# A hybrid encoder layer on one core: attention-branch products and gates moved into the scan, elimination steps respread, and the last pair's sum made in PSUM

## The reference, cut to what matters

```python
h = rmsnorm(x, norm1_g) * (1.0 + sc1) + sh1
q, k, v, feat, gl = split(h @ w_in)
att = windowed_attention(q, k, v, attn_sink) @ w_br_attn
rw = rwkv7_bidir(feat, ...) @ w_br_rwkv          # forward scan + backward scan, group norm, bonus, * g
g_att, g_rw = split(sigmoid(gl))
x = x + gt1 * ((g_att * att + g_rw * rw) @ w_out)
h = rmsnorm(x, norm2_g) * (1.0 + sc2) + sh2
moe = expert_choice_moe(h, ...)                  # 16 experts, each takes its 64 best tokens
x = x + gt2 * moe
return rmsnorm(x, final_g)
```

## Time and profile before

| | us |
|---|---|
| three runs | 1594.44, 1598.31, 1598.44 (median 1598.31) |
| profiled execution | 1594.55, span 1592.7 |
| mean granted TensorE clock | 0.962 of 2.4 GHz |
| PE / DVE / ACT / POOL busy | 1402.1 / 467.1 / 205.3 / 39.1 |
| moved by DMA | 485.52 MB |

### The profile page before, as it was taken

How to read it: one execution, slowest core, us unless ns; L and a number is a source line. 1 busy time by engine, 2 the same in 40 slices (tenths; PEclk the granted TensorE clock), 3 DMA queues, 4 the chain that set the end, 5 groups by cost and what they waited for, 6 DMA issues and landing times.

```text
span 1592.7 us, 21565 instructions
## 1 busy us (share of the span) xinstructions
PE 1402.1 (88%) x9239; PEld 663.4 (42%) x9239; DVE 467.1 (29%) x807; ACT 205.3 (13%) x401; POOL 39.1 (2%) x45
## 2 busy tenths in 40 slices
PE   5988999899778998799979889989889989889886
PEld 1433544445676444434334343344343343343332
DVE  3799643762237323310200200200200200201103
ACT  2024001122223002101001001001010010010002
POOL 2003030000000000000000000000000000000000
PEclk9998999999899999799999999999999999999998
DMA  9951242144402173799999999999999999999995
GB/s 346 374 174 58 80 106 63 56 135 118 174 5 112 76 279 127 279 428 429 427 428 429 428 428 429 428 428 428 428 430 428 429 429 428 428 429 428 428 428 209
DMA packets 91267, 485.52 MB, mean 305 GB/s; under 512 B 36075, under 2 KB 53565, under 8 KB 62405
## 3 DMA queue, kind: packets, MB, share of 16 engines
q1 hardware_dynamic: 91149, 484.59, 74.8%
q10 hardware_dynamic: 56, 0.01, 0.0%
HBM read 470.93 MB, written 10.50 MB: 302 GB/s over the span
## 4 chain that ended last, share of the span: by engine, by line
PE 57%; DMA 29%; DVE 8%; issue 3%; POOL 1%; ACT 1%; SPq 1%; DVEq 0%; PEldq 0%; POOLq 0%
PE psum L1111 16%; DMA arena<-in_exp_w_up_dram 14%; DMA arena<-in_exp_w_gate_dram 12%; PE psum L1126 8%; PE psum L694 6%; PE psum L581 5%; PE psum L1092 4%; DMA arena<-in_ada_w_dram 4%; PE psum L997 3%; PE psum L1027 3%; PE psum L1200 2%; DVE arena L1611 1%; PE psum L709 1%; DVE arena L1479 1%; DVE inv_tmp L1609 1%
## 5 line engine op out<-in xcount | busy, mean ns | idle before, releaser
L1111 PE MATMUL psum<-arena 128*64 128x512 f32 x2048 | 474.2, 620 | 81.2 <-DMA arena<-in_exp_w_up_dram 62.3
L1111 PEld LDWEIGHTS psum<-arena 128*64 128x64 f32 x2048 | 165.8, 142 | 382.7 <-issue 382.4
L1126 PE MATMUL psum<-arena 128*64 128x512 f32 x992 | 217.5, 596 | 11.2 <-issue 9.4
L581 PE MATMUL psum<-arena 128*128 128x512 f32 x336 | 149.1, 605 | 1.4 <-DVE arena L1505 1.4
L1126 PEld LDWEIGHTS psum<-arena 128*64 128x64 f32 x992 | 83.5, 138 | 139.5 <-issue 139.3
L694 PE MATMUL psum<-arena 128*128 128x512 f32 x256 | 124.5, 610 | 0.0
L581 PEld LDWEIGHTS psum<-arena 128*128 128x128 f32 x336 | 64.5, 194 | 84.2 <-issue 80.6
L1881 DVE TENSOR_TENSOR arena<-arena,psum 128x512 f32<-128x512 f32 x32 | 19.8, 681 | 268.5 <-PE psum L1111 268.5
L1896 DVE TENSOR_TENSOR arena<-psum,arena 128x1024 f32<-128x1024 f32 x7 | 8.6, 1225 | 251.3 <-PE psum L1126 251.3
L1873 DVE TENSOR_TENSOR arena<-arena,psum 128x512 f32<-128x512 f32 x32 | 19.8, 681 | 169.3 <-ACT arena L1422 169.3
L1413 ACT ACTIVATE arena<-psum,arena 128x128 f32<-128x128 f32 x64 | 24.3, 457 | 328.6 <-PE psum L1092 328.6
(11 more groups left out here) (269 smaller groups left out, 1067.7 us busy)
## 6 DMA issues: line engine op xcount, KB each, us to landing
arena<-in_exp_w_gate_dram SPq DMA_DIRECT2D x64, 2048.0 KB, 24.5
arena<-in_exp_w_up_dram SPq DMA_DIRECT2D x64, 2048.0 KB, 26.7
arena<-in_exp_w_down_dram SPq DMA_DIRECT2D x62, 2048.0 KB, 26.9
arena<-in_ada_w_dram SPq DMA_DIRECT2D x24, 1024.0 KB, 9.9
arena<-in_w_in_dram SPq DMA_DIRECT2D x16, 1024.0 KB, 5.8
arena<-in_x_dram SPq DMA_DIRECT2D x2, 2048.0 KB, 8.5
gate_pre<-arena SPq DMA_DIRECT2D x16, 256.0 KB, 6.1
arena<-in_w_out_dram SPq DMA_DIRECT2D x1, 4096.0 KB, 20.9
```

The source lines that it names most:

```text
L581: ins = mm(bank(b % 4), by(w_ring[g % 2], KC)[:, k, j * P:(j + 1) * P], by(hT, KC)[:, k, :], start=(k == 0), stop=(k == KC - 1))
L1111: ins = mm(bank(4 * kind + n)[e * 64:(e + 1) * 64, :], by(xeT, KC)[:, k, e * 64:(e + 1) * 64], by(ring[(j + e) % RING], 2)[:, r, n * 512:( ...
L1126: ins = mm(bank(4 + n)[e * 64:(e + 1) * 64, :], by(hidT, FBLK)[:, 4 * kk + b, e * 64:(e + 1) * 64], by(ring[(j + e) % RING], 4)[:, b, n * ...
```

## The change

Seven things move.

1. Projection block 9 stands ahead of the sums of `kk` squares instead of behind them.
2. The triangle products of both directions are made together, two banks for each pair of chunks, and two gate products follow each of the four groups. Each query block then has 24 gate products; the heads of block q are turned inside block q+1, after its second pair of scores.
3. The elimination steps are spread over 24 places: four in the logits and eight in the heads of blocks 1 and 2.
4. In the scan both directions turn their keys through bank 6, so bank 7 is free. `att_branch` makes one attention-branch product at four places in each of steps 1 to 7, and four behind the scan. VectorE multiplies each block by its gate in place (`att_gated`), and ScalarE takes the sigmoids of the attention gates in steps 1 and 2.
5. `w_br_rwkv` goes to another place in SBUF and is loaded once the last `C` products (step 6 of the scan) are made, ahead of the second gate half; `g_spill` is loaded ahead of both.
6. Behind the scan the rwkv branch is made for the middle chunks first ("inner"), then for the outer ones; the mix has two operations a block instead of three.
7. In the last pair, tiles 0 to 2 of `x2` are put into PSUM by products with the identity; the put products add to them, and norm and final product read PSUM. Tile 3 is first and is summed by VectorE as before.

The diff, cut:

```diff
-        wba, wbr = at(136, 16 * KB), at(64, 16 * KB)
+        wba, wbr = at(136, 16 * KB), at(32, 16 * KB)
         wo = at(0, 32 * KB)
-        mix_tmp = [at(40, T), at(42, T)]
+        mix_tmp = at(64, T)
...
+            load(GG, g_spill, "g_moved")
+            sp.wait_ge(sem("C_mm"), 2 * STEPS)
+            sp.wait_ge(sem("N_mm"), 2 * STEPS - 2)
+            load(by(wbr, 4), w_br_rwkv[0].rearrange("(k p) n -> p k n", p=P), "wbr_in")
             load(by(gate_half[1], KC)[:, 0:4, :], gate_rows[:, KC:KC + 4, :], "gates_in")
-            load(GG, g_spill, "g_moved")
             sp.wait_ge(sem("Y_mm"), STEPS)
             load(by(gate_half[1], KC)[:, 4:KC, :], gate_rows[:, KC + 4:GATEB, :], "gates_in")
-            load(by(wbr, 4), w_br_rwkv[0].rearrange("(k p) n -> p k n", p=P), "wbr_in")
...
-            for b in range(7, 9):
+            for b in range(7, 10):
                 project(b)
             pe.wait_ge(sem("lora_out"), 19)
             pe.wait_ge(sem("kk_sq"), 1)
             for m in range(PAIRS):
                 ins = mm(bank(6)[m * 32:(m + 1) * 32, :], half_wide, by(kk_sq, PAIRS)[:, m, :], start=True, stop=True)
             ins.then_inc(sem("kk_sum"), 1)
-            for b in range(9, 12):
+            for b in range(10, 12):
...
+            def a_product(d, n, c, m, h):
+                left, right = ((al_, be_), (be_, al_))[d]
+                p = 1 - h if d == 0 else h
+                o = (c % 2 * PAIRS + m) * CHUNK
+                return mm(bank(4 + (2 * n + d) % 4)[head(p), o:o + CHUNK], left[head(h), d, m, token(c)],
+                          right[head(h), d, m, token(c)], start=True, stop=True)
+            pe.wait_ge(sem("v_nat_out"), 5)
+            for n in range(4):
+                if n >= 2:
+                    pe.wait_ge(sem("A_made"), 2 * n - 2)
+                for c in (2 * n, 2 * n + 1):
+                    for m in range(PAIRS):
+                        for h in range(2):
+                            a0 = a_product(0, n, c, m, h)
+                            a1 = a_product(1, n, c, m, h)
+                a0.then_inc(sem("A_mm"), 1)
+                a1.then_inc(sem("A_mm"), 1)
+                if n == 0:
+                    pe.wait_ge(sem("shift_done"), 13)
+                gate_products(2 * n, 2 * n + 2)
...
-                g0 = 26 * q
+                g0 = 8 + 24 * q
+                ahead, doubled = ((6, 2), (6, 2), (6, 2), (4, 0))[q]
-                gate_products(g0 + 8, g0 + 14)
+                    if q and j == 1:
+                        heads_turned(q - 1)
+                gate_products(g0 + 8, g0 + 8 + ahead)
+                g0 += 8 + ahead
...
-                    gate_products(g0 + 14 + h, g0 + 15 + h)
+                    more = 2 if h < doubled else 1
+                    gate_products(g0, g0 + more)
+                    g0 += more
-                gate_products(g0 + 22, g0 + 26)
-                pe.wait_ge(sem("o_ready"), q + 1)
-                if q:
-                    pe.wait_ge(sem("attT_ready"), q)
-                for m in range(4):
-                    ins = nc.tensor.transpose(bank(7)[:, m * P:(m + 1) * P], o_nat[:, m * P:(m + 1) * P], ident)
-                ins.then_inc(sem("attT_mm"), 1)
+            gate_products(100, 104)
+            heads_turned(TT - 1)
...
-                return mm(cell(6 + d, slot(h, d), m, 256 * n), (be_, ka_)[n][head(h), d, m, token(chunk(i, d))],
+                return mm(cell(6, slot(h, d), m, 256 * n), (be_, ka_)[n][head(h), d, m, token(chunk(i, d))],
...
+            def att_branch(b, m, k):
+                if k == 0 and b == 7 and m:
+                    pe.wait_ge(sem("mixT_ready"), m)
+                ins = mm(bank(b), by(wba, 4)[:, k, m * P:(m + 1) * P], by(attT, 4)[:, k, :], start=(k == 0), stop=(k == 3))
+                if k == 3:
+                    ins.then_inc(sem("mix_mm"), 1)
             Bq(0)
+            transposed(0, 0)
             for i in range(STEPS):
                 last = i == STEPS - 1
                 if i:
                     W_with_C(i, last)
                 else:
                     C(1, 0)
+                    transposed(0, 1)
                 if not last:
                     Bq(i + 1)
+                if i == 1:
+                    pe.wait_ge(sem("wba_in"), 16)
+                if i:
+                    att_branch(7, i - 1, 0)
                 U(i, 1)
                 U(i, 0)
                 if not last:
                     C_with_turns(i + 1)
                 if i > 5:
                     gn_transposed(i - 2)
+                if i:
+                    att_branch(7, i - 1, 1)
                 if not last:
                     SU(i)
+                if i:
+                    att_branch(7, i - 1, 2)
                 Y(i)
                 if i < STEPS - 2:
                     transposed(i + 1, 1)
+                if i:
+                    att_branch(7, i - 1, 3)
...
+            def rw_branch(m, cols):
                 for k in range(4):
+                    b, left = bank(RWB[m]), by(wbr, 4)[:, k, m * P:(m + 1) * P]
+                    if cols == "inner":
+                        ins = mm(b[:, 2 * CHUNK:6 * CHUNK], left, rw_in[:, k, 2:6], start=(k == 0), stop=(k == 3))
+                    elif cols == "all":
+                        ins = mm(b, left, rw_in[:, k], start=(k == 0), stop=(k == 3))
+                    else:
+                        for e in range(2):
+                            o = 6 * e
+                            ins = mm(b[:, o * CHUNK:(o + 2) * CHUNK], left, rw_in[:, k, o:o + 2],
+                                     start=(k == 0 and e == 0), stop=(k == 3 and e == 1))
                 return ins
+            for k in range(4):
+                att_branch(5, 7, k)
             gn_transposed(6)
+            pe.wait_ge(sem("Y_out"), STEPS)
+            pe.wait_ge(sem("wbr_in"), 16)
+            pe.wait_ge(sem("gn_out"), 2)
+            for m in range(3):
+                rw_branch(m, "inner")
             gn_transposed(7)
+            rw_branch(3, "inner")
+            pe.wait_ge(sem("gn_out"), 3)
+            rw_branch(4, "inner")
             pe.wait_ge(sem("gn_out"), 4)
             for m in range(KC):
+                if m > 5:
+                    pe.wait_ge(sem("mixT_ready"), m + 1)
+                rw_branch(m, "outer" if m < 5 else "all").then_inc(sem("mix_mm"), 1)
...
+            def x2_placed(t):
+                for n in range(2):
+                    mm(bank(LAST_BANK[t] + n), ident, by(x2, TT)[:, t, n * 512:(n + 1) * 512], start=True, stop=False)
...
+                    if last and kk < 2:
+                        x2_placed(kk)
...
+                    pe.wait_ge(sem("put_ready"), i + 1)
+                    x2_placed(2)
                     last_narrow(i)
-                    pe.wait_ge(sem("put_ready"), i + 1)
-                    for n in range(2):
-                        pe.wait_ge(sem("ye_ready"), i + 1 + n)
-                        for t in range(TT):
-                            mm(bank((6, 0, 1, 2, 3, 4, 5, 7)[n * TT + t]), put[:, t * P:(t + 1) * P],
-                               ye[:, n * 512:(n + 1) * 512], start=True, stop=True).then_inc(sem("put_mm"), 1)
+                    for t in LAST_TILES:
+                        for n in range(2):
+                            if t == LAST_TILES[0]:
+                                pe.wait_ge(sem("ye_ready"), i + 1 + n)
+                            mm(bank(LAST_BANK[t] + n), put[:, t * P:(t + 1) * P], ye[:, n * 512:(n + 1) * 512],
+                               start=(t == LAST_TILES[0]), stop=True).then_inc(sem("put_mm"), 1)
...
+                if i in (1, 2):
+                    act.wait_ge(sem("gates_in"), 16)
+                    gate_sigmoid(0, i - 1)
...
+            def inverse(k):
+                if k == 0:
+                    dve.wait_ge(sem("tri_in"), 16)
+                lo = 2 * k + 1 if k < 4 else k + 4 if k < 21 else 2 * k - 17
+                for i in range(lo, lo + (2 if k < 3 or k > 20 else 1)):
+                    invert(i)
...
+                    if q in (1, 2) and n % 2:
+                        inverse(12 * (q - 1) + n // 2)
...
+            def att_gated(m, b):
+                dve.wait_ge(sem("gate_ready"), 1 + m // 4)
+                dve.wait_ge(sem("mix_mm"), m + 1)
+                v.tensor_tensor(ga[:, m, :], ga[:, m, :], bank(b), ALU.mult).then_inc(sem("mixT_ready"), 1)
+                if i > 1:
+                    att_gated(i - 2, 7)
...
-                s(v.tensor_tensor(mix_tmp[0], ga[:, m, :], bank(m if m < 6 else m - 4), ALU.mult))
-                s(v.tensor_tensor(mix_tmp[1], gr[:, m, :], bank(6 + m % 2), ALU.mult))
-                v.tensor_tensor(by(mixT, KC)[:, m, :], mix_tmp[0], mix_tmp[1], ALU.add).then_inc(sem("mixT_ready"), 1)
+                dve.wait_ge(sem("mix_mm"), KC + m + 1)
+                dve.wait_ge(sem("gate_ready"), 3 + m // 4)
+                dve.wait_ge(sem("mixT_ready"), KC + m)
```

(4 more changed lines are left out.)

162 lines of the change are left out of this document (67 added, 95 removed).

## The result

The changed kernel takes **1578.69 us** in the median of 4 runs (1576.83 to 1580.04), the kernel before 1597.19 us in 4 runs (1594.44 to 1598.44). The ratio is 0.988, with a 95% interval from 0.9865 to 0.9900: faster by 1.0 to 1.35%. The profiled execution has a span of 1576.3 us, against 1592.7 before.

The account below looks back on a forecast made before the run. Expert stage fixed by weight transfers at some 902 us, TensorE the spine ahead of it; terms +2.2 - 11.5 + 15.6 - 22.1 - 1.8 = -17.6 from 1594.55 us gave 1577, predicted 1578 us, range 1568 to 1590.

Parts of the forecast that it names:

- Block 9: Projections: block 9 fills an earlier wait, TensorE idles from about 143 to 150.4 us, block 12 starts at half clock: +2.2 us.
- Triangles and attention: Triangle products and query blocks: stalls, the first-logits wait and most waits for VectorE's copies go: -11.5 us, bounds -13.5 and -4.
- the new order reaches the first scores at 218 + 14.4: Attention: with 3.7 us of bonus, first scores come at 236 us, after POOL's end at 234.4, so that wait goes.
- Scan: Scan stage: 28 branch products, sigmoids, clock loss and loads lengthen it by 15.6 us, bounds +5 and +27.
- the load under steps 6 and 7: Scan steps 6 and 7: w_br_rwkv and a gate load may slow the program's pieces: +3 us.
- sigmoids and clock (7): Scan steps 1 and 2: sigmoids and table load ahead of the y copy +5.0 us, half clock afterwards +2.
- B: Rival, scan: gaps are not program fetch and stay; products cost 19.8 us instead of 5.4; 1591 us, chance 0.14.
- Behind the scan: Scan's end to output projection: 35.6 us instead of 57.7, gain 22.1 us; the last normed chunks set the outer parts' start.
- Tail: Last pair: placements save 1.4 us in a gap and add 2.5, the shorter end saves 2.9: sum -1.8 us.
- C: Rival, attention: elimination steps outlast their slots or POOL sets the pace; -4 instead of -11.5, 1585 us, chance 0.12.
- D: Rival, scan steps 1 to 7: TensorE falls to 1.2 GHz and stays, +8 us a step; slower, chance 0.05.
- E: Rival: all better, no clock loss, no slow piece, sigmoids partly hidden; -26, 1568 us, chance 0.09.

## Why the forecast held, and where it did not

**Block 9**: right in kind (a full slot emptied a later one, then the lower clock) and in size: 2.1 us against 2.2. The other 0.4 of the 2.5 lie ahead of it, where nothing was changed.

**Triangles and attention**: the copies' waits went, even the 1.0 us that I had kept, and a new wait of 1.6 us for later logits came in their place. What I had not seen is in "the new order reaches the first scores at 218 + 14.4". The 256 triangle records of the kernel before, in two halves by direction, were these:

```profile
L671 PE MATMUL psum<-arena 64*64 64x64 f32 x256 | 7.8, 219 | 1.2 <-issue 1.2
```

and in the kernel after, where the directions alternate, these:

```profile
L681 PE MATMUL psum<-arena 64*64 64x64 f32 x256 | 4.6, 221 | 0.0
```

I had taken the old pace of the products for the new order. 64 records start within 0.95 us now (15 ns apart), and 213 took 6.06 us before (28 ns). That is 3.2 of the 4.4 us; a product of one direction and its twin of the other read the same half of the partitions and write to different halves, so that all four pairings of input and output half now take turns instead of two. The run with the order undone has the old pace again (7.8 us). I think that more of them run in the array at once, but no run took that alone: the two directions also write to different banks in turn, which the old order did not. The clock loss that was to vanish with POOL's wait did.

**Scan**: the step that failed is "So in steps 1 to 6 a product group costs about 0.4 to 0.8 us, step 7, which has no gaps, 2.9: together 5.4 us". With the sigmoids out of the way the scan is still 14.4 us longer than before: 1.7 less in step 0, 4.0 more in step 1, 7.1 in steps 2 to 6, 5.0 in step 7. Step 0 has no branch product; its gap was 3.5 us instead of 4.3, and its clock 1.00 in that trace and 0.81 before. I had compared the sum of 8.32 and 3.44 us with the step's 11.34 and so priced each product at 0.86; it takes 1.13 to 1.20 there, and TensorE is busy for 12.3 of the 12.3 us in step 4. Once the gaps are full, each further 0.1 us counts. In step 7 the added wait for the gated product, which I had not looked for, took 1.5 us. On the other side stands the load under steps 6 and 7, priced at 3 us and worth nothing. So 5.4 should have been 14 to 16 and 3 should have been 0, while sigmoids and clock (7) were 6.1. That the scan's error was met by one of nearly the same size in the attention is luck. Of the rivals, B had the cost of the products nearer (19.8) with the wrong mechanism: the gaps that it said would stay did not stay.

**Behind the scan**: 33.9 us behind all 28 products, against 35.6 forecast. The last normed chunks did not set the start of the outer parts, as the forecast had it: VectorE was done with them at 526.45 us, and TensorE went from the last inner product to the first outer one at 527.1 us without a gap. It was busy through the whole stretch, so the length is that of its own work.

**Output projection to the experts**: +1.6 us that no term had. The same stretch took 92.8 to 94.3 us in the other runs, which don't differ in it. TensorE runs about a quarter of it at the lower clock, 23.9 us before and 27.3 us after. The runs fall in two groups by this: 23.9 us at the lower clock go with 92.8 to 93.0 us (three traces), 27.3 us with 93.8 to 94.3 (ten). So the 1.6 us are 3.4 us more at half clock, and not a thing of the change that any run shows; I leave open what decides between the two.

**Tail**: -2.2 from the stages and -1.1 when undone, against -1.8. Against the kernel before the steps came as forecast: the gap of 2.70 us shrank to 0.81, the 32 records behind it took 7.09 us instead of 8.53, and the put products start 1.1 us later. But in the run with the old tail the same 32 records took 7.09 us too, behind a gap of 2.69, so the 1.4 us that the placement was to save are not lost in every execution. The shorter end paid 3.3 us, a little more than the 2.9 of the forecast.

Of the rivals, C (no attention gain) fell at the waits, D (slower by the clock) at the clock of 0.88 to 0.89 in steps 1 to 3 and 1.00 from step 4 on, and E (all better) at the sigmoids and the clock behind them, which cost 6.1 us.

## What to carry to other kernels

Work put into an engine's gaps costs its own time less the gap, and its own time must be taken in its new surroundings: price a large product between small ones at its spacing there, and put such products in pairs ahead of the place where the engine runs dry. Before moving work into a wait, ask what it leaves empty behind it. Before placing work on a helper engine ahead of a copy that others wait for, look for its idle stretch in the same loop: here it was 5.5 us long and one instruction further up.

## What the runs showed of the hardware

- A single 128x512 fp32 product between 64x64 ones takes 1.20 us of TensorE at full clock, in a row of such products 0.86 us.
- 64x64 products that take turns over all four pairings of input and output half of the partitions start 15 ns apart, over two pairings 28 ns (256 records: 4.6 against 7.8 us busy). The faster order also alternates between two banks, and no run parts the two.
- TensorE's program comes in packets of 16 KB, one for about 128 records of products, 3.4 to 3.8 us apart at the densest and 6.0 to 6.4 us apart under 320 GB/s; a step of 385 records in 10.6 to 11.8 us runs dry in the middle, the same with 3.4 us of long products rightly placed hardly does (stops of 0.6 and 0.9 us in seven steps, besides those ahead of a step).
- A stop of 7.2 us was followed by a granted clock of 0.56, and the stop of 3.45 us behind step 1 by records at half clock for 3.4 us.
